# A chunked recurrence: the inverse from 32x32 blocks, heads in swapped halves, group norm on 128 partitions

## The chip, the cores and the metric

The kernel is one program on one core of a Trainium2 chip. The metric is the device time of one execution in microseconds (us); a run gives the median of its timed executions. All data are float32.

## The reference, cut to what matters

The program computes two transformer-like blocks for 256 tokens of width 1024. Only one layer of the first block is touched, a time mixing with 16 heads of 64 features. Per head it runs this recurrence over the tokens, then normalises each head's output, adds a bonus term and gates it:

```
state = state * w_t + (state @ -kk_t) (kk_t * a_t)' + v_t k_t'
y_t   = state @ r_t
yn    = (y - mean) * rsqrt(var + LNX_EPS) * lnx_w + lnx_b      (mean, var over each head's 64 features)
out   = ((yn + (sum(r * k * r_k)) * v) * g) @ w_o
```

## The kernel before

`rwkv()` works on four chunks of 64 tokens (`NCH`, `CHUNK`). 16 heads are held as 8 pairs m, with g = 0, 1 for the head of a pair, which takes partitions 0 to 63 or 64 to 127 (`half(g)`). Two blocks of code follow each other. The first (up to L1393) makes the operands: `ARs` (per pair and chunk a window w = 0 with the decayed -kk and w = 1 with r), `BKs` (w = 0 with kk*a, w = 1 with k), the values in `UV[64:128]`, `bonus`. The second (L1396 to L1715) is the recurrence, with an instruction list written out by hand for each engine; semaphores (`wait`) tie them together.

In the second block TensorE (PE) does for chunk c:

- `products` (L1455): all inner products of the chunk for each head, a 128x128 block (L1463), which VectorE (DVE) masks into `G` (L1647), and one more 64x64 product (L1469), masked into `NT[0]` (L1650). With N the strictly triangular 64x64 part of it, (I - N) has to be inverted.
- `power(c, j, q)` (L1473): the inverse as a product of (I + N^(2^j)). For j = 0 to 4 the powers N and their transposes are squared, 64x64 (L1485), and copied back by ScalarE (ACT, L1587); for j = 1 to 5 the running product X is multiplied by them (L1493) and DVE adds (L1662). q is one of two groups of four pairs, so that one group's copies run beside the other group's matmuls. The last X is `XF`.
- `values` (L1498): G's lower half times the values, 64 rows by 128 columns (L1502).
- in the body of chunk c: transposes of BK (L1524), the state's part of the right side (L1532), `products(c + 1)`, then u = XF times R (L1542), which ACT copies (L1603), y (L1550), which ACT copies to `Y` (L1610), and the new state (L1554), which DVE adds and decays (L1683, L1684).
- `z_turn` (L1506): the normalised outputs of the chunk before, turned back to features; DVE gates them (L1666).

The powers of chunk c + 1 are written in between, so PE has work while ACT and DVE handle chunk c. The group norm of chunk c (L1687 to L1714) is on DVE, interleaved with the `add_x` of chunk c + 1, on 64 partitions with 1024 elements each, since all tokens' outputs lie on partitions 64 to 127; ACT does the squares (L1616) and the root (L1621). ACT also copies the transposed N (`begin_at`, L1579).

A float32 matmul of the code leaves two MATMUL records in the trace and a transpose one: 16 matmuls of a `power` are x32.

Of the kernel before, what the change touches and what calls it, by code (L numbers as in the profile page):

```python
# [88 lines left out]
def build_program(nc, d, out):  # L89
    with ExitStack() as ctx:  # L90
# [16 lines left out]
        bonus = sb("bonus", [P, NCH, HEADS])  # L107
# [1046 lines left out]
        def rwkv():  # L1154
# [31 lines left out]

            def by_chunk(x):
                return x.rearrange("p m (c s) -> p m c s", c=NCH)
# [4 lines left out]
            with new_block() as block:  # L1193
# [8 lines left out]
                def _(dve):  # L1202
# [39 lines left out]
                    for f in range(2):  # L1242
                        dve.tensor_tensor(ARs[f][:, :, :, 1, :], two_chunks(rx, f), two_chunks(scratch, f), ALU.mult)
# [11 lines left out]
                    for f in range(2):  # L1255
                        dve.scalar_tensor_tensor(ARs[f][:, :, :, 0, :], two_chunks(kk, f), -1.0, two_chunks(sgm, f), ALU.mult, ALU.mult).then_inc(exp_used.up(), 1)
                    dve.wait_ge(exp_used.sem, exp_used.at(2))
                    dve.tensor_tensor(BKs[:, :, :, 0, :], by_chunk(ax), by_chunk(kk), ALU.mult)
                    dve.wait_ge(bonus_mm.sem, bonus_mm.at(1))
                    dve.tensor_copy(bonus[64:128].rearrange("p c a -> p (c a)"), bank(4)[64:128, 0:NCH * HEADS])  # L1260

                @block.tensor
                def _(pe):
# [68 lines left out]
                    for c in range(NCH):  # L1332
                        for m in range(KD):
                            last = pe.matmul(bank(4)[64:128, c * HEADS + 2 * m:c * HEADS + 2 * m + 2], xT[:, m, c * CHUNK:(c + 1) * CHUNK], pair, start=True, stop=True)
# [5 lines left out]
                def _(act):  # L1340
# [23 lines left out]
                    def copy_values(u):  # L1364
                        for t in range(T):
                            src = product(V_OUT + 2 * u + t)
                            for half in range(2):
                                o = UV[64:128, 2 * t + half, :, 4 * u:4 * u + 4, :].rearrange("p g m v -> p m g v")
                                ins = act.copy(o, src[64 * half:64 * half + 64, :].rearrange("p (m g v) -> p m g v", m=4, g=2))
# [21 lines left out]
                    act.wait_ge(exp_used.sem, exp_used.at(2))  # L1391
                    act.copy(BKs[:, :, :, 1, :], by_chunk(kx))
# [8 lines left out]
            NT = [blk(5)[:, i * 1024:(i + 1) * 1024].rearrange("p (m w s) -> p m w s", m=KD, w=2) for i in range(2)]  # L1401
            X = [spare[:, i * 512:i * 512 + 512].rearrange("p (m s) -> p m s", m=KD) for i in range(2)]
            R = spare[:, 1024:1536].rearrange("p (m v) -> p m v", m=KD)
            XF = spare[:, 1536:2048].rearrange("p (m s) -> p m s", m=KD)
            Y = blk(2)[64:128, 1024:2048]
            Z = blk(8)[64:128, 0:1024]
            W1 = blk(8)[64:128, 1024:2048]
            ST = mask.rearrange("p t s -> p (t s)").rearrange("p (m v) -> p m v", m=KD)
            POWERS = 5
# [9 lines left out]
            def half(g):  # L1419
# [1203 lines left out]
```

## Time and profile before

| | |
|---|---|
| median of 3 runs | 1875.41 us (1873.86 to 1875.72) |
| the profiled execution | 1868.42 us, its span 1866.8 us |
| PE, DVE, ACT busy | 1741.7, 957.2, 718.0 us |
| first block of `rwkv()` ends, recurrence begins | 477.25 us |
| recurrence ends, the next projection begins | 614.44 us |

The page gives the busy time of each engine; the timeline lists instructions in order of time, equal ones merged; the table of stretches gives busy times and the clock that TensorE was granted (1.00 is 2.4 GHz, 0.50 is 1.2 GHz). A matmul's record lasts about 0.22 us of which most overlaps with its neighbours, so the pace of a run of them is read from (merged time - one record) / (records - 1).

### The profile page before, as it was taken

The numbers are of one execution on the slowest core, as the hardware profiler recorded it, in microseconds if no ns is written. First come the engines' busy times: TensorE is split into PE (matmuls) and PEld (weight loads), VectorE is DVE, ScalarE is ACT, GpSimd is POOL, SyncE is SP. The second block draws the span as 40 slices with busy tenths as digits, with TensorE's granted clock in tenths as the row PEclk, the third lists the DMA queues.
The fourth block names the chain that finished last, engine by engine and source line by source line (L and its number), as shares of the span: only waits on it lengthen the run. The fifth ranks groups of instructions, "written<-read, shape, count | busy, mean of one in ns | idle before, by whom it ended". The sixth has DMA issues, their size and how long they took to land. (4 is left out here: it accounts for less than half of the span.)

```text
span 1866.8 us, 30841 instructions
## 1 busy us (share of the span) xinstructions
PE 1741.7 (93%) x12958; PEld 1372.5 (74%) x12958; DVE 957.2 (51%) x1947; ACT 718.0 (38%) x1322; POOL 0.2 (0%) x4
## 2 busy tenths in 40 slices
PE   8999999999997889999998999999978899999995
PEld 6778999786797789998787877555544688855553
DVE  6566556734376755567556755222223665713213
ACT  4465445323343444445546543111122454411111
POOL 0000000000000000000000000000000000000000
PEclk9999999999998899999999999999988999999998
DMA  7512454334000534543450435999962134499995
GB/s 309 226 62 98 180 203 158 110 136 158 25 3 2 214 125 178 203 146 125 163 198 20 161 147 195 423 425 426 423 292 90 46 113 158 156 418 425 424 426 229
DMA packets 34286, 374.34 MB, mean 201 GB/s; under 512 B 4944, under 2 KB 6096, under 8 KB 9568
## 3 DMA queue, kind: packets, MB, share of 16 engines
q1 hardware_dynamic: 30096, 362.51, 48.6%
q10 hardware_dynamic: 4048, 9.80, 1.6%
q8 instruction: 106, 1.74, 0.4%
q14 instruction: 36, 0.29, 0.0%
HBM read 371.25 MB, written 1.05 MB: 199 GB/s over the span
## 5 line engine op out<-in xcount | busy, mean ns | idle before, releaser
L1993 PE MATMUL ps<-ring,expert_inputs 128*64 128x256 f32 x2048 | 235.1, 382 | 7.7 <-DMA ring<-in_w_moe 7.7
L519 ACT CAST w_h<-ring 128x512 fp32r<-128x512 f32 x256 | 157.1, 622 | 140.0 <-PE ps L527 126.8
L522 DVE TENSOR_TENSOR w_l<-ring,w_h 128x512 fp32r<-128x512 f32 x256 | 172.4, 690 | 74.8 <-ACT w_h L519 72.3
L527 PE MATMUL ps<-ffn_x_h,ffn_w_h 128*128 128x256 f32 x704 | 201.3, 286 | 10.1 <-DVE ffn_w_l L522 9.9
L527 PE MATMUL ps<-ffn_x_l,ffn_w_h 128*128 128x256 f32 x704 | 200.5, 285 | 0.0
L527 PE MATMUL ps<-ffn_x_h,ffn_w_l 128*128 128x256 f32 x704 | 200.5, 285 | 0.0
L1993 PEld LDWEIGHTS ps<-ring,expert_inputs 128*64 128x64 f32 x2048 | 141.4, 137 | 77.4 <-DMA ring<-in_w_moe 8.8
L527 PE MATMUL ps<-w_h,x_h 128*128 128x512 f32 x416 | 163.6, 393 | 5.5 <-DVE w_l L522 5.5
L522 DVE TENSOR_TENSOR ffn_w_l<-ring,ffn_w_h 128x1024 fp32r<-128x1024 f32 x132 | 155.5, 1221 | 22.3 <-ACT ffn_w_h L519 22.3
L527 PE MATMUL ps<-w_h,x_l 128*128 128x512 f32 x416 | 162.0, 389 | 0.0
L527 PE MATMUL ps<-w_l,x_h 128*128 128x512 f32 x416 | 162.0, 389 | 0.0
L148 PE MATMUL ps<-ident 128*128 128x256 f32 x470 | 122.3, 409 | 33.4 <-PEq L2451 5.6
L519 ACT CAST ffn_w_h<-ring 128x1024 fp32r<-128x1024 f32 x132 | 131.2, 1045 | 37.7 <-PE ps L527 23.0
L527 PEld LDWEIGHTS ps<-ffn_x_h,ffn_w_h 128*128 128x128 f32 x704 | 136.5, 194 | 11.7 <-DVE ffn_w_l L522 10.9
L527 PEld LDWEIGHTS ps<-ffn_x_l,ffn_w_h 128*128 128x128 f32 x704 | 136.4, 194 | 0.8
L527 PEld LDWEIGHTS ps<-ffn_x_h,ffn_w_l 128*128 128x128 f32 x704 | 136.4, 194 | 0.0
L148 PEld LDWEIGHTS ps<-ident 128*128 128x128 f32 x470 | 92.3, 204 | 54.3 <-issue 41.7
L2121 ACT ACTIVATE routing<-ps 64x256 f32<-64x256 f32 x64 | 24.1, 376 | 279.3 <-PE ps L1993 279.3
L2245 DVE TENSOR_TENSOR routing<-routing,ps 64x256 f32<-64x256 f32 x64 | 27.2, 424 | 193.5 <-ACT routing L2121 193.3
L2016 PE MATMUL ps<-ring,routing 128*64 128x512 f32 x512 | 122.3, 598 | 0.8 <-DVE routing L2253 0.8
L527 PEld LDWEIGHTS ps<-w_h,x_h 128*128 128x128 f32 x416 | 78.1, 188 | 24.7 <-DVE w_l L522 5.1
L527 PEld LDWEIGHTS ps<-w_h,x_l 128*128 128x128 f32 x416 | 78.1, 188 | 16.3
(348 smaller groups left out, 2864.9 us busy)
## 6 DMA issues: line engine op xcount, KB each, us to landing
ring<-in_w_moe SPq DMA_DIRECT2D x64, 2048.0 KB, 14.4
ring<-in_w_proj SPq DMA_DIRECT2D x37, 2048.0 KB, 8.0
ring<-in_w_ffn SPq DMA_DIRECT2D x22, 3072.0 KB, 10.1
ring<-in_w_moe SPq DMA_DIRECT2D x64, 1024.0 KB, 16.0
rows<-in_ln_g ACTq DMA_DIRECT2D x6, 512.0 KB, 3.6
rows<-in_ln_b ACTq DMA_DIRECT2D x6, 512.0 KB, 5.3
ring<-in_w_b_in SPq DMA_DIRECT2D x1, 2496.0 KB, 19.2
ring<-in_w_lora SPq DMA_DIRECT2D x1, 2048.0 KB, 7.9
```

Of the source, the lines that this page charges most:

```text
L148: pe.matmul(bank(b)[:, 0:2 * P].rearrange("p (o f) -> p o f", o=2), ident[:], wide, start=True, stop=True, skip_group_check=True)
L519: act.copy(high, x).then_inc(ready.up(), 1)
L522: return dve.tensor_tensor(low, x, high.bitcast(F32), ALU.subtract)
L527: last = pe.matmul(out, a[x], b[y], start=start and n == 0, stop=stop and n == 2, skip_group_check=True)
L1993: last = pe.matmul(bank(0)[g * SLOTS_E:(g + 1) * SLOTS_E, 0:2 * P], x[:, k, e * SLOTS_E:(e + 1) * SLOTS_E], wg[:, g, k, :], start=(k == 0) ...
L2016: last = pe.matmul(bank(2)[c * SLOTS_E:(c + 1) * SLOTS_E, :], hids[:, f, :], wd[:, f, c * 512:(c + 1) * 512], start=(n % 2 == 0 and f == 0 ...
L2121: act.activation(sg[SLOTS_E:2 * SLOTS_E, :], bank(0)[0:SLOTS_E, 0:2 * P], ACT.Silu).then_inc(silu_done.up(), 1)
L2245: dve.tensor_tensor(hid_tok[up, :], sg[up, :], bank(0)[up, 0:2 * P], ALU.mult).then_inc(hid_made.up(), 1)
```

## The change

- In the first block `BKs`, `ARs` and the values are written so that for g = 1 the two windows and the two halves are swapped: the recurrence then has head g's N on partitions `half(g)` for both heads, and the values on `half(1 - g)`. An instruction that wrote all partitions becomes two that write 64.
- N is split in two 32x32 diagonal blocks (b = 0, 1) and one block below. `power` squares only the diagonal blocks, for j = 0 to 3 (`POWERS` = 4), as 32x32 matmuls, four for each pair (`sub(g, b)`); X is 32x32 too. `low` makes one product of the block below with the upper inverse and copies of it (L1543, L1544), ACT copies it (`copy_low`), `inverse` multiplies by the lower inverse (L1551), and ACT and DVE copy the results into `XF`. `products(c + 1)` and u now wait for these copies.
- `begin_at` goes: j = 0 reads `G` and `N0` in place. Two masks are made by six small ACT copies at the start.
- `values`, y and `z_turn` alternate between the halves; `values` comes after the last power. `z_turn` becomes 16 matmuls of 64x64 in place of 8 transposes.
- Y, W1 and Z have 128 partitions with 512 elements; the small rows of the group norm follow, and lnx_w and lnx_b come by four DMAs.
- The last chunk leaves out its transposes and its new state.

The diff, cut to its core:
```diff
-                                ins = act.copy(o, src[64 * half:64 * half + 64, :].rearrange("p (m g v) -> p m g v", m=4, g=2))
+                            for part in range(2):
+                                x = src[half(part), :].rearrange("p (m g v) -> p m g v", m=4, g=2)
+                                for g in range(2):
+                                    ins = act.copy(UV[half(1 - g), 2 * t + part, g, 4 * u:4 * u + 4, :], x[:, :, g, :])
                             ins.then_inc(evac.up(), 1)
...
-            POWERS = 5
+            gms = [gm, rows[:, 0, 512:640]]
+            eye = sin0.rearrange("p t f -> p (t f)")[:, CHUNK:CHUNK + SUB]
+            lnx = [rows[:, i, 0:512] for i in range(2)]
+            POWERS = 4
...
-                        for q in range(2):
-                            if c:
-                                pe.wait_ge(x_added[q].sem, x_added[q].at(POWERS * c))
+                        if c:
+                            for copied, count in inverse_copied(c - 1):
+                                pe.wait_ge(copied.sem, count)
...
+                        tiles = [(m, m % GROUP, g, b) for m in range(GROUP * q, GROUP * (q + 1)) for g in range(2) for b in range(2)]
                         if j < POWERS:
-                            for m in range(GROUP * q, GROUP * (q + 1)):
-                                i = m % GROUP
-                                for w in range(2 if j < POWERS - 1 else 1):
-                                    for g in range(2):
-                                        last = pe.matmul(nt_out(q)[half(g), i, w, :], nt[half(g), m, 1 - w, :], nt[half(g), m, w, :], start=True, stop=True)
+                            for w in range(2 if j < POWERS - 1 else 1):
+                                for m, i, g, b in tiles:
+                                    x = operands(c, j, m, g, b)
+                                    last = pe.matmul(nt_out(q)[sub(g, b), i, w, :], x[1 - w], x[w], start=True, stop=True)
                             last.then_inc(powers_ready[q].up(), 1)
...
+                            for m, i, g, b in tiles:
+                                last = pe.matmul(x_out(q)[sub(g, b), i, :], NT[j % 2][sub(g, b), m, 0, :], X[j % 2][sub(g, b), m, :], start=True, stop=True)
...
+                    def low(c, q):
+
+                        pe.wait_ge(x_added[q].sem, x_added[q].at(POWERS * (c + 1)))
+                        if c == 0:
+                            wait(pe, "masks_made", 2)
+                        for m, i, g in heads_of(q):
+                            pe.matmul(inv_out(q)[sub(g, 0), i, half_cols(0)], XF[sub(g, 0), m, half_cols(1)], eye[sub(g, 0), :], start=True, stop=True)
+                            last = pe.matmul(low_out(q)[sub(g, 1), i, :], before(c, g)[sub(g, 0), m, half_cols(1)], XF[sub(g, 0), m, half_cols(1)], start=True, stop=True)
+                        last.then_inc(low_ready.up(), 1)
+
+                    def inverse(c, q):
+
+                        pe.wait_ge(act_out.sem, low_copied(c, q))
+                        for m, i, g in heads_of(q):
+                            last = pe.matmul(inv_out(q)[sub(g, 0), i, half_cols(1)], LOW[sub(g, 1), m, :], XF[sub(g, 1), m, half_cols(1)], start=True, stop=True)
+                        last.then_inc(inv_made.up(), 1)
...
-                        for g in range(2):
-                            for m in range(KD):
-                                last = pe.matmul(bank(VY + g)[:, m * 64:(m + 1) * 64], G[c % 2][64:128, g, m, :], UV[64:128, c, g, m, :],
+                        for m in range(KD):
+                            for g in range(2):
+                                last = pe.matmul(bank(VY + g)[:, m * 64:(m + 1) * 64], G[c % 2][half(1 - g), g, m, :], UV[half(1 - g), c, g, m, :],
...
-                        for m in range(KD):
-                            last = pe.transpose(bank(M_BANK)[:, m * CHUNK:(m + 1) * CHUNK], Z[:, m * P:(m + 1) * P], ident[64:128, 64:128])
+                        for m, i, g in ALL:
+                            last = pe.matmul(bank(M_BANK)[half(g), m * CHUNK:(m + 1) * CHUNK], Z[half(1 - g), m * HD:(m + 1) * HD], ident[half(1 - g), half(1 - g)], start=True, stop=True)
...
+                    def last_power(c):
+                        for q in range(2):
+                            power(c, POWERS, q)
+                        values(c)
+                        for q in range(2):
+                            low(c, q)
...
-                        for m in range(KD):
+                        for m in range(KD if ahead else 0):
...
+                        for q in range(2):
+                            inverse(c, q)
                         if ahead:
+                            wait(pe, "bk_copied", 2 * c + 2)
                             products(c + 1)
...
+                        for m, i, g in ALL:
+                            last = pe.matmul(bank(VY + g)[half(1 - g), m * 64:(m + 1) * 64], G[c % 2][half(g), g, m, half(1 - g)], UV[half(g), c, g, m, :],
...
+                            act.wait_ge(low_ready.sem, low_ready.at(2 * c + q + 1))
+                            for g in range(2):
+                                ins = act.copy(LOW[sub(g, 1), pairs(q), :], low_out(q)[sub(g, 1)])
+                            ins.then_inc(act_out.up(), 1)
...
-                        begin_at(c + 1, 0)
+                        for q in range(2):
+                            act.wait_ge(inv_made.sem, inv_made.at(2 * c + q + 1))
+                            act.copy(XF[sub(0, 0), pairs(q), :], inv_out(q)[sub(0, 0)]).then_inc(act_out.up(), 1)
...
+                            dve.tensor_tensor(N0[:, pairs(q), :], by_pair(bank(M_BANK))[:, pairs(q), :], wide_l, ALU.mult).then_inc(n["an_begun"].up(), 1)
+                        wait(dve, "g_masked", 4 * c + 4)
+                        wait(dve, "an_begun", 2 * c + 2)
+                        for g in range(2):
+                            for b in range(2):
+                                x = before(c, g) if b else N0
+                                ins = dve.tensor_tensor(X[1][sub(g, b)], x[sub(g, b), :, half_cols(b)], wide_i[sub(g, b)], ALU.add)
+                        ins.then_inc(n["x_begun"].up(), 1)
...
-                        o = (XF if j == POWERS else X[(j + 1) % 2])[:, pairs(q), :]
+                        o = XF[:, pairs(q), half_cols(1)] if j == POWERS else X[(j + 1) % 2][:, pairs(q), :]
                         dve.tensor_tensor(o, X[j % 2][:, pairs(q), :], x_out(q), ALU.add).then_inc(x_added[q].up(), 1)
...
+                        for q in range(2):
+                            dve.wait_ge(inv_made.sem, inv_made.at(2 * c + q + 1))
+                            dve.tensor_copy(XF[sub(1, 0), pairs(q), :], inv_out(q)[sub(1, 0)]).then_inc(dve_out.up(), 1)
...
                         add_x(c + 1, 2, 0)
+                        add_x(c + 1, 2, 1)
                         dve.wait_ge(sig("squares_ready").sem, sig("squares_ready").at(c + 1))
-                        step(dve.tensor_reduce(sm, rows3(W1), AX, ALU.add))
-                        add_x(c + 1, 2, 1)
-                        dve.tensor_scalar(stat[64:128, 16:32], sm, 1.0 / HD, LNX_EPS, ALU.mult, ALU.add).then_inc(sig("mean_square").up(), 1)
+                        step(dve.tensor_reduce(sm, by_pair(W1), AX, ALU.add))
                         add_x(c + 1, 3, 0)
+                        dve.tensor_scalar(stat[:, 16:24], sm, 1.0 / HD, LNX_EPS, ALU.mult, ALU.add).then_inc(sig("mean_square").up(), 1)
+                        add_x(c + 1, 3, 1)
...
-                        step(dve.tensor_tensor(W1, W1, rows[64:128, 1, :], ALU.add))
                         add_x(c + 1, 4, 0)
+                        add_x(c + 1, 4, 1)
+                        step(dve.tensor_tensor(W1, W1, lnx[1], ALU.add))
                         dve.wait_ge(sig("row_root").sem, sig("row_root").at(c + 1))
```

PE, the powers of chunk 1 (before) and of chunk 0 (now): L1485 and L1526 square, L1493 and L1534 multiply X.

```order
L1485 MATMUL ps<-arena_7 64x64 x16
L1493 MATMUL ps<-ring,arena_7 64x64 x8
L1485 MATMUL ps<-arena_7 64x64 x16
L1493 MATMUL ps<-ring,arena_7 64x64 x8
L1485 MATMUL ps<-arena_7 64x64 x8
```

```order
L1526 MATMUL ps<-arena_7 32x32 x32
L1534 MATMUL ps<-ring,arena_7 32x32 x16
L1526 MATMUL ps<-arena_7 32x32 x32
L1534 MATMUL ps<-ring,arena_7 32x32 x16
L1526 MATMUL ps<-arena_7 32x32 x16
```

Each step has twice as many matmuls, of a quarter of the size, and there is one step fewer.

PE, from the end of chunk 1's powers to u of chunk 1: the first piece is before (L1502 is `values`, L1524 the transposes, L1532 the state's part, L1463 and L1469 `products`, L1542 u), the second is now (L1543 and L1544 `low`, L1551 `inverse`).

```order
L1502 MATMUL ps<-arena_8,arena_0 128x64 x16
L1493 MATMUL ps<-ring,arena_7 64x64 x16
L1524 MATMUL ps<-ident,arena_7 128x128 x8
L1532 MATMUL ps<-mask,ring 128x64 x16
L1463 MATMUL ps<-ring,arena_7 128x128 x8
L1469 MATMUL ps<-arena_7,ring 64x64 x16
L1463 MATMUL ps<-ring,arena_7 128x128 x8
L1542 MATMUL ps<-ring 64x64 x16
```

```order
L1543 MATMUL ps<-sin,ring 32x32
L1544 MATMUL ps<-ring,arena_0 32x32
L1586 MATMUL ps<-ident,arena_7 128x128 x8
L1594 MATMUL ps<-mask,ring 128x64 x16
L1551 MATMUL ps<-ring,arena_7 32x32 x16
L1497 MATMUL ps<-ring,arena_7 128x128 x8
L1503 MATMUL ps<-arena_7,ring 64x64 x16
L1497 MATMUL ps<-ring,arena_7 128x128 x8
L1607 MATMUL ps<-ring 64x64 x16
```

`inverse` stands between the state's part and the products, which wait for the copies of what it made; the pair L1543, L1544 comes 16 times.

ACT in the same place and on to Y: before (L1597 copies the transposes, L1599 R, L1579 `begin_at`, L1603 u, L1587 the powers, L1610 Y), and now (L1649 `copy_low`, L1672 the new copies into `XF`).

```order
L1597 COPY arena_0<-ps 128x512 x2
L1599 COPY ring<-ps 64x512
L1579 COPY arena_7<-arena_0 64x4x64 x2
L1603 COPY arena_8<-ps 64x512 x2
L1579 COPY arena_7<-arena_0 64x4x64 x2
L1587 COPY arena_7<-ps 128x512
L1610 COPY arena_0<-ps 64x8x64 x2
```

```order
L1649 COPY arena_7<-ps 32x128 x4
L1667 COPY arena_0<-ps 128x512 x2
L1669 COPY ring<-ps 64x512
L1672 COPY ring<-ps 32x256 x2
L1675 COPY arena_8<-ps 64x512 x2
L1641 COPY arena_7<-ps 128x256
L1681 COPY arena_0<-ps 64x512 x2
```

Two short copies of `XF` stand behind R's; the copies of the powers have half the elements.

## Rows read from the trace of the kernel before

**Rows 1.** Page, section 1: busy us (share of the span) x instructions.

```profile
PE 1741.7 (93%) x12958; PEld 1372.5 (74%) x12958; DVE 957.2 (51%) x1947; ACT 718.0 (38%) x1322; POOL 0.2 (0%) x4
```

**Rows 2.** Busy time, granted clock, DMA by stretch: prologue, three chunks, last chunk.

```profile
477.25:499.00 21.75, 20.62 (x545) 19.93 (x545) 8.54 (x19) 7.05 (x14) 0.00 (x0) 1.00 0.14 51
499.00:527.55 28.55, 26.71 (x651) 25.36 (x649) 18.47 (x33) 13.07 (x24) 0.00 (x0) 0.98 0.01 3
527.55:557.33 29.78, 29.43 (x690) 28.03 (x689) 22.12 (x36) 12.10 (x23) 0.00 (x0) 0.96 0.01 3
557.33:587.36 30.03, 29.68 (x690) 28.33 (x688) 21.98 (x36) 12.10 (x23) 0.00 (x0) 0.95 0.02 4
587.36:614.44 27.08, 11.41 (x156) 10.42 (x152) 16.77 (x21) 5.14 (x9) 0.00 (x0) 0.63 0.00 1
```

**Rows 3.** Groups of instructions by line, 475 to 615 us: busy, mean ns | idle before.

```profile
L1485 PE MATMUL ps<-arena 64*64 64x64 f32 x1152 | 40.1, 219 | 1.9 <-ACT arena L1579 1.0 <-ACT arena L1587 0.7
L1493 PE MATMUL ps<-ring,arena 64*64 64x64 f32 x640 | 25.7, 223 | 0.0
L1587 ACT COPY arena<-ps 128x256 f32<-128x256 f32 x8 | 3.0, 373 | 3.2 <-PE ps L1485 3.2
```

**Rows 4.** Timeline of the first two bodies: start us, us, engine, line, operation.

```profile
506.51 2.07 PE L1550 MATMUL ps<-arena,arena 64*64 64x64 f32 x32 [0.35 <-ACT arena L1603]
...
508.51 1.15 PE L1554 MATMUL ps<-arena,arena 128*64 128x64 f32 x32
...
509.60 2.08 PE L1485 MATMUL ps<-arena 64*64 64x64 f32 x64
...
522.13 3.78 PE L1502 MATMUL ps<-arena,arena 64*128 64x64 f32 x32
...
527.55 1.97 PE L1524 MATMUL ps<-ident,arena 128*128 128x128 f32 x8
...
529.45 2.03 PE L1532 MATMUL ps<-mask,ring 64*128 64x64 f32 x32
...
531.52 0.58 ACT L1599 COPY ring<-ps 64x512 f32<-64x512 f32 x1 [1.39 <-PE ps L1532]
```

**Rows 5.** PE in windows of 10 ns: matmuls then in flight (x).

```profile
482.84:482.85 0.01, 0.00 (x0) 1.00 0.00 0
482.86:482.87 0.01, 0.01 (x2) 1.00 0.00 0
...
483.03:483.04 0.01, 0.01 (x6) 1.00 0.00 0
...
483.09:483.10 0.01, 0.01 (x8) 1.00 0.00 0
```

**Rows 6.** Stretches at half clock (same columns as rows 2).

```profile
526.10:529.50 3.40, 3.40 (x42) 2.95 (x36) 2.19 (x4) 0.59 (x1) 0.00 (x0) 0.50 0.00 0
...
594.40:614.40 20.00, 6.64 (x74) 6.05 (x71) 13.10 (x16) 2.33 (x4) 0.00 (x0) 0.50 0.00 1
```

**Rows 7.** Timeline of the last chunk.

```profile
587.37 1.09 PE L1524 MATMUL ps<-ident,arena 128*128 128x128 f32 x8
...
593.80 3.21 PE L1550 MATMUL ps<-arena,arena 64*64 64x64 f32 x32 [1.27 <-ACT arena L1603]
...
597.04 1.06 ACT L1610 COPY arena<-ps 64x512 f32<-64x512 f32 x2 [3.30 <-PE ps L1550]
...
600.40 1.22 DVE L1687 TENSOR_REDUCE stat<-arena 64x16 f32<-64x1024 f32 x1
...
612.28 1.08 PE L1509 MATMUL ps<-ident,arena 64*128 64x64 f32 x8 [12.32 <-DVE arena L1714]
```

**Rows 8.** Timeline around the seam of the two blocks of `rwkv()`.

```profile
475.75 1.17 ACT L1369 COPY arena<-ps 64x512 f32<-64x512 f32 x2 [5.70 <-PE ps L1296]
...
477.28 1.16 PE L1463 MATMUL ps<-ring,arena 64*128 64x128 f32 x16 [1.57 <-PEq L1193]
...
478.56 1.29 DVE L1647 TENSOR_TENSOR arena<-ps,cos 128x512 f32<-128x512 f32 x2 [18.20 <-PE ps L1463]
```

More of the change, by code:

```diff
@@ L1390, in _ @@
                     copy_values(0)
-                    act.wait_ge(exp_used.sem, exp_used.at(2))
-                    act.copy(BKs[:, :, :, 1, :], by_chunk(kx))
+                    act.wait_ge(exp_used.sem, exp_used.at(4))
+                    for g in range(2):
+                        act.copy(BKs[half(g), :, :, 1 - g, :], by_chunk(kx)[half(g)])
                     copy_values(1)
@@ L1450, in _ @@
                 def _(sp):
-                    sp.dma_start(rows[:, 0, :], d["lnx_w"].rearrange("(o f) -> o f", o=1).broadcast_to([P, D])).then_inc(c_in.up(16), 16)
-                    sp.dma_start(rows[:, 1, :], d["lnx_b"].rearrange("(o f) -> o f", o=1).broadcast_to([P, D])).then_inc(c_in.up(16), 16)
+                    for i, x in enumerate((d["lnx_w"], d["lnx_b"])):
+                        by_half = x.rearrange("(o m g v) -> o g m v", o=1, m=KD, g=2)
+                        for g in range(2):
+                            sp.dma_start(by_pair(lnx[i])[half(1 - g)], by_half[:, g].broadcast_to([64, KD, HD])).then_inc(c_in.up(16), 16)
                 @block.tensor
@@ L1515, in _ @@
                             power(0, j, q)
[L1516 to L1519 removed]
+                    last_power(0)
                     for c in range(NCH):
                         ahead = c + 1 < NCH
[L1523 removed]
+                        for m in range(KD if ahead else 0):
                             last = pe.transpose(bank(NT_BANK + m // 4)[:, (m % 4) * P:(m % 4 + 1) * P], BK(m, c), ident[:])
@@ L1565, in _ @@
                                     power(c + 1, j, q)
-                            values(c + 1)
-                            for q in range(2):
-                                power(c + 1, POWERS, q)
+                            last_power(c + 1)
                     wait(pe, "z_gated", NCH - 1)
@@ L1573, in _ @@
                 def _(act):
-                    def begin_at(c, q):
-                        if c == NCH:
-                            return
-                        wait(act, "g_masked", 4 * c + 2 * q + 2)
-                        for g in range(2):
-                            ins = act.copy(NT[0][half(g), pairs(q), 1, :], G[c % 2][0:64, g, pairs(q), 0:64])
-                        ins.then_inc(n["at_begun"].up(), 1)
                     def copy_powers(c, j, q):
@@ L1593, in _ @@
                             copy_powers(0, j, q)
+                    copy_low(0)
                     for c in range(NCH):
-                        for f in range(2):
+                        for f in range(2 if c + 1 < NCH else 0):
                             wait(act, "bk_turned", 2 * c + f + 1)
@@ L1666, in gate @@
                         dve.tensor_tensor(xT[:, :, c * CHUNK:(c + 1) * CHUNK], by_pair(bank(M_BANK)), gT[:, :, c * CHUNK:(c + 1) * CHUNK], ALU.mult).then_inc(n["z_gated"].up(), 1)
+                    for g in range(2):
+                        ins = dve.memset(XF[sub(g, 1), :, half_cols(0)], 0.0)
+                    step(ins)
                     dve.wait_ge(masks_in.sem, masks_in.count)
+                    wait(dve, "masks_made", 2)
                     begin(0)
```

173 lines of the change are left out of this document (92 added, 81 removed).

## The prediction

> **What bounds the kernel now.** I read the page first: TensorE (PE) is busy 93% of the span, DVE 51%, ACT 38% [rows 1]. Then the table of stretches, since the change lies in one stage of 137 us, 477.25 to 614.44. Its prologue takes 21.75 us and its three full chunks 28.55, 29.78 and 30.03 us, mean 29.45; in the full chunks PE is busy all but 0.4 us or so of each later stretch, and DMA moves next to nothing [rows 2]. The last 27 us are another case: PE is busy 11.4 of them and DVE 16.8. So the chunks are bound by how fast PE takes the small matmuls, and the last one by a chain through DVE. Before the stage ends nothing later can start, and the stages behind it keep their lengths: I take what the stage gains or loses as the kernel's.
>
> **Pace of the matmuls.** The trace has 1152 + 640 records of the powers [rows 3], 448 a chunk, 224 matmuls of the code. 64 records of alternating halves take 2.08 us: (2.08 - 0.22) / 63 = 29.5 ns a record, 59 ns a matmul. Where all matmuls use the same rows (y, L1550), (2.07 - 0.22) / 31 = 60 ns a record; so two halves of the array work side by side and each keeps 60 ns. With 128 columns of weights, one half alone takes (3.78 - 0.27) / 31 = 113 ns a record (`values`), alternating halves (2.03 - 0.27) / 31 = 57 [rows 4]. The narrow windows show that after a wait two matmuls are in flight within the same 20 ns, and from then on two more every 60 ns: 2, 6, 8 in flight [rows 5]. The start of a second half costs the first nothing.
>
> **The powers.** Now there are 2 x 176 = 352 matmuls of 32x32 a chunk, with `low` and `inverse` 400, at a price s that the trace doesn't show. From below: a 32x32 record should hold its part of the array for half of 60 ns, and with four parts side by side a matmul (two records) costs 2 x 30 / 4 = 15 ns. A middle price is 30 ns, if the second record of one matmul has to follow its first before the next part may start. From above 59 ns, since no two matmuls of the code follow each other faster anywhere in the stage. 13.2 us (224 x 59) become 6.0, 12.0 or 23.6 us. I take 20 ns, 8.0 us: nearer to the lower end because of rows 5, above it because `low` and `inverse` use two parts only. That is -5.2 us a chunk.
>
> **The rest of a full chunk.** (1) `values` goes from 3.78 to the 2.03 of L1532, -1.8; y from 2.07 to about 1.15 as L1554, -0.95 [rows 4]. (2) `z_turn`: 8 records of some 0.1 become 32 at 30 ns, +0.4. (3) After `values` the clock falls to 0.50 for 3.4 us [rows 6]; 8 transposes then take 1.97 us [rows 4] and not 1.09 [rows 7]. With both halves busy I expect this in fewer chunks, -1.0. (4) A new wait: `inverse` must be copied before `products(c + 1)`. ACT has R's copy (0.58, [rows 4]) ahead of two short copies, for which I take 0.3 each, below the 0.37 of 128x256 [rows 3]; PE meanwhile had only `inverse` itself, and its whole stream stands behind the wait. +1.1. `copy_low` is covered by the transposes and the state's part, 3 us; without that cover it would cost 0.9. (5) Changes of matmul shape: L1554 starts at 508.51 and at 30 ns a record would hand over at 509.47; L1485 starts at 509.60 [rows 4], 0.1 us later than in a run of equal shape. Some seven more such changes, +0.7. (6) Between u and y PE waits 0.35 us for ACT's copies although a `power` fills the gap [rows 4]; a shorter `power` leaves 0.3 more, and the chain of copies and DVE steps between powers may show another 0.3: +0.6. ACT's `begin_at` is gone and the copies of powers are 0.37 in place of 0.59; DVE loses half of eight norm steps; both engines have room (18 to 22 and 13 of 29 us busy, [rows 2]), so I cost that at nothing, covered by PE's matmuls; if PE fell under DVE's 18 us of work, DVE would be next. Sum: -5.2 - 1.8 - 0.95 + 0.4 - 1.0 + 1.1 + 0.7 + 0.6 = -6.15, a chunk of 23.3 us; three are -18.5.
>
> **The prologue.** -5.2 and -1.8 as above, -1.0 for `begin_at`, +0.5 for the chain, +0.3 for the six copies that make the masks (they lie beside `products(0)`): -7.2.
>
> **The last chunk.** No transposes, but the inverse's wait: -0.6. y at half clock takes 3.21 us on one half [rows 7]; alternating, half of it: -1.5. DVE's first norm step starts at 600.40, though the second copy of Y ends at 598.10, since the state's two steps stand before it: they go, -2.3. The norm has seven steps of 64x1024 at 1.22 us [rows 7]; 128x512 takes 0.65 (half of 1.29, [rows 8]); seven times 0.55 and 0.4 for the square: -4.2. `z_turn` at half clock: +0.7. Sum -7.9; PE waits 12.32 us for this chain [rows 7].
>
> **The first block.** Split writes double some DVE and ACT steps, and BKs' copy. DVE is idle for 18.20 us before its first step of the recurrence, so some 7 us more are hidden; ACT's last copies (two of 0.58 ending at 476.92, [rows 8]) become four shorter ones, +0.5 on the path. The four DMAs of lnx_w and lnx_b have short pieces but are wanted only 15 us after they are issued: nothing.
>
> **Sum.** -18.5 - 7.2 - 7.9 + 0.5 = -33.1 us against the profiled execution (1868.42 us, 1.6 around its span), which lies 7.0 below the median; the same difference from the median 1875.4 gives **1842 us**.
>
> **Other prices of s.** At 15 ns a full chunk is -7.5 and the prologue -8: 1837 us. At 30 ns -2.75 and -3.7: -8.3 - 3.7 - 7.4 = -19.4, 1856 us. The sum is zero near 43 ns.
>
> The windows show two parts starting together, and no more can be seen in this kernel. The Trainium skill (TensorE: Matmul & The Clock Gate, Part 3, The mechanism) says that small parts of the array run concurrently with starts some 4 ns apart; rows 5 agree for two parts. By it alone s would be the 15 ns above, and the time 1837 us.
>
> **Rivals.** (a) *PE takes no more than one matmul per 59 ns*, whatever its size: what limits it is taking instructions, not the array. For it: no closer pace in 1792 records, and 59 is also what two halves would give, so the trace can't tell. Against it: after a wait two matmuls start together. Powers, `low` and `inverse` then cost 23.6 us, +10.4; with (1), (2), (3), (4), (5) and 1.2 us of waits that vanish behind the longer stream, a chunk is +7.6, three +22.8; the prologue +7.9; the last chunk and the seam -7.4: +23.3, **1899 us**. It decides from 43 ns on. The Trainium skill (TensorEngine Tiling (Array Packing), Instruction Overhead) speaks for this side: each matmul has an overhead of about 60 cycles, and one should not take a tiling factor from a dimension that is already small. An estimate from that page is 25 ns a record at 2.4 GHz, and 50 ns a matmul if both records pay it, near 1885 us; no run here shows it for 32 columns. (b) *The clock stays at 0.50 in the chunks*, since short matmuls with waits between them keep PE less busy: the last chunk runs so [rows 6]. Work like the transposes then takes 1.8 times as long; some 17 us of a chunk are PE's, +14 each, which gives 1842 + 42 + 10 = 1894 us. (c) *The chain, not PE, bounds the new chunk*: each power needs PE, ACT's copy and back, and DVE's additions stand behind norm steps. It would hold a chunk at 26 to 27 us: 1853 us. (d) The change doing less than it says, such as half of the tiles side by side: s = 30, 1856 us.
>
> **How the numbers follow.** Forecast (s from 15 to 25 ns) 0.42, its own range 1832 to 1850; (c) or (d) 0.22; (a) with its milder form at 50 ns 0.29; (b) 0.05; the rest 0.02. The predicted time is the forecast's, 1842. The range must leave out no more than 2 in 10: from 1830 (15 ns and no half clock) to 1892, which takes in the milder part of (a). Within 0.2% (about what a measurement of this kernel can tell) is 1871.7 to 1879.2 us: 0.04. Faster 0.65, slower 0.31.
>
> **What would show it.** The 32x32 matmuls of L1526 closer than 15 ns a record; full chunks of 22 to 25 us; a wait of about 1 us before L1497 with ACT's L1672 as its end; `values` at 57 ns a record and no half clock behind it; the norm steps at 0.65 to 0.69 us; PE's wait before the last `z_turn` some 7 us shorter. I am wrong if L1526 keeps 29 ns a record, or if the chunks show half clock.

## The result: 23 us slower, and the profile after

The changed kernel takes 1897.59 us (median of 4, 1895.54 to 1901.58); the kernel before took 1874.63 us beside it. The ratio is 1.0127, 95% interval 1.0107 to 1.0147. The prediction of 1842 us, range 1830 to 1892, had the wrong sign and a range that doesn't hold the time. The profiled execution has a span of 1893.7 us. Page, section 1, answers to [rows 1]:

```profile
PE 1738.7 (92%) x14486; PEld 1366.7 (72%) x14486; DVE 943.2 (50%) x1952; ACT 708.9 (37%) x1335; POOL 0.2 (0%) x4
```

PE has 1528 records more and is busy 3 us less. The stage, cut at the same places as in [rows 2] (prologue, three full chunks, last chunk; the columns are the same, the clock is the number before the last two):

```profile
476.14:503.15 27.01, 19.09 (x865) 17.54 (x865) 8.55 (x21) 4.16 (x16) 0.00 (x0) 0.64 0.10 23
503.15:537.41 34.26, 25.41 (x1006) 23.36 (x1000) 15.04 (x33) 10.29 (x25) 0.00 (x0) 0.65 0.01 4
537.41:577.18 39.77, 30.44 (x1071) 28.09 (x1065) 16.91 (x36) 9.31 (x24) 0.00 (x0) 0.67 0.01 4
577.18:617.04 39.86, 31.16 (x1071) 28.65 (x1064) 16.99 (x36) 9.29 (x24) 0.00 (x0) 0.63 0.01 3
617.04:639.86 22.82, 12.31 (x200) 11.57 (x193) 9.52 (x17) 5.23 (x13) 0.00 (x0) 0.50 0.01 2
```

The stage takes 163.7 us in place of 137.2. Against [rows 2] the prologue is +5.3, the chunks are +5.7, +10.0 and +9.8, the last chunk is -4.3. Two columns tell how. PE, which was busy all but 0.4 us of a later chunk, now stands still for 9 us of it, and the granted clock is 0.63 to 0.67 where it was 0.95 to 0.98. The groups of PE in the stage, against [rows 3]:

```profile
L1526 PE MATMUL ps<-arena 32*32 32x32 f32 x1280 | 22.0, 217 | 16.3 <-issue 16.3
L1534 PE MATMUL ps<-ring,arena 32*32 32x32 f32 x1024 | 20.6, 228 | 12.0 <-issue 11.3 <-DVE ring L1723 0.5
L1560 PE MATMUL ps<-arena,arena 64*128 64x64 f32 x128 | 14.7, 421 | 0.0
L1497 PE MATMUL ps<-ring,arena 64*128 64x128 f32 x128 | 13.2, 365 | 3.9 <-PEq L1196 1.9 <-DVE ring L1752 1.2 <-ACT ring L1672 0.7
L1594 PE MATMUL ps<-mask,ring 64*128 64x64 f32 x96 | 11.0, 421 | 0.0
```

The idle time lies before the 32x32 matmuls of the powers, 27.6 us of it with "issue" as its end: PE waited for no engine, no semaphore and no data that the profile shows. Here is one such piece of the first full chunk in narrow stretches:

```profile
517.90:519.00 1.10, 1.06 (x120) 1.06 (x121) 0.00 (x0) 0.36 (x1) 0.00 (x0) 1.00 0.06 15
...
520.00:521.30 1.30, 0.00 (x0) 0.00 (x0) 0.00 (x0) 0.00 (x0) 0.00 (x0) 0.91 0.00 0
521.30:522.40 1.10, 1.00 (x76) 1.00 (x79) 0.00 (x0) 0.37 (x1) 0.00 (x0) 0.50 0.00 0
522.40:523.30 0.90, 0.90 (x71) 0.79 (x60) 0.83 (x2) 0.00 (x0) 0.00 (x0) 0.50 0.08 18
523.30:525.10 1.80, 0.02 (x3) 0.00 (x0) 0.07 (x1) 0.89 (x2) 0.00 (x0) 0.50 0.00 0
525.10:526.20 1.10, 1.08 (x81) 1.07 (x84) 0.29 (x1) 0.00 (x0) 0.00 (x0) 0.50 0.00 0
526.20:527.20 1.00, 0.85 (x64) 0.72 (x56) 0.22 (x2) 0.37 (x1) 0.00 (x0) 0.50 0.06 16
527.20:528.50 1.30, 0.00 (x0) 0.00 (x0) 0.67 (x2) 0.00 (x0) 0.00 (x0) 0.50 0.00 0
```

At clock 1.00, 120 records start in 1.10 us: 9 ns a record, 18 ns a matmul. So the array takes the new matmuls as cheaply as predicted. But after a burst comes a pause in which no engine's work is awaited, and with each burst one transfer (18 GB/s for 0.9 us, 16 KB). The queue that it belongs to, in the window 477 to 620 us, first of the kernel after, then of the kernel before:

```profile
q8 instruction: 32, 0.52, 1.4%
```

```profile
q8 instruction: 21, 0.34, 1.0%
```

Each packet is 0.52 MB / 32 = 16 KB of instructions. Cut at the ends of the stage itself, the queue has 33 packets after and 21 before. Bursts begin at 521.39, 525.12 and 528.58, one batch apart.

The other reading is of the wait before `products` and of the last chunk (timeline):

```profile
539.31 3.68 PE L1594 MATMUL ps<-mask,ring 64*128 64x64 f32 x32
...
543.60 0.79 ACT L1672 COPY ring<-ps 32x256 f32<-32x256 f32 x2
543.65 0.80 DVE L1752 COPY ring<-ps 32x256 f32<-32x256 f32 x2
...
544.60 2.08 PE L1497 MATMUL ps<-ring,arena 64*128 64x128 f32 x16 [0.61 <-DVE ring L1752]
...
636.77 1.98 PE L1567 MATMUL ps<-ident,arena 64*64 64x64 f32 x32 [7.46 <-DVE arena L1789]
```

The rhs matmuls of L1594, 2.03 us in [rows 4], take 3.68 at half clock. The wait for the inverse's copies is there. Here it ends with DVE's copy, at 544.45, just after ACT's at 544.39; of the three waits of the stage (0.6 to 0.7 us each) two end with DVE's copy and one with ACT's L1672. The wait before the last `z_turn` is 7.46 in place of 12.32 [rows 7].

### The profile page after: what moved, and what is told of

It reads as the page before. It is cut to its first block and busy times, and to the rows that moved or that the text cites. A ratio compares the mean times of both kernels' runs of the same rounds, so it can differ in the third digit from the quotient of the medians.

```text
span 1893.7 us, 33918 instructions
## 1 busy us (share of the span) xinstructions
PE 1738.7 (92%) x14486; PEld 1366.7 (72%) x14486; DVE 943.2 (50%) x1952; ACT 708.9 (37%) x1335; POOL 0.2 (0%) x4
## 5 line engine op out<-in xcount | busy, mean ns | idle before, releaser
L527 PE MATMUL ps<-ffn_x_h,ffn_w_h 128*128 128x256 f32 x704 | 201.4, 286 | 10.1 <-DVE ffn_w_l L522 9.8
L527 PE MATMUL ps<-w_h,x_h 128*128 128x512 f32 x416 | 163.7, 394 | 6.7 <-DVE w_l L522 6.7
L527 PEld LDWEIGHTS ps<-ffn_x_h,ffn_w_h 128*128 128x128 f32 x704 | 136.4, 194 | 11.6 <-DVE ffn_w_l L522 10.9
## 6 DMA issues: line engine op xcount, KB each, us to landing
ring<-in_w_moe SPq DMA_DIRECT2D x64, 2048.0 KB, 14.7
ring<-in_w_ffn SPq DMA_DIRECT2D x22, 3072.0 KB, 10.1
```

The source lines that it names most:

```text
L527: last = pe.matmul(out, a[x], b[y], start=start and n == 0, stop=stop and n == 2, skip_group_check=True)
```

## The experiments

Two theories: **supply** (PE gets its instructions in batches of 16 KB, one per 3.45 us or more, which 64 float32 matmuls use up) and **clock** (half clock makes the wide matmuls of a chunk slower, and is a loss of its own). The rival of the first is a fixed price for each matmul.

### The price of the small matmuls by itself

```diff
+for k in range(384):                        # before products(0)
+    r = slice(32 * (k % 4), 32 * (k % 4) + 32)
+    pe.matmul(spare_bank[r, 0:32], ident[r, 0:32], ident[r, 0:32], ...)
+# the same with 64 columns; then 64x64 on two halves, 64 columns
```

> The kernel before, with three runs of matmuls put ahead of the recurrence's first product, 384 each, none waiting for anything: 32x32 on four parts with 32 columns (L1515), the same with 64 columns (L1518), and 64x64 on two halves with 64 columns (L1521). Supply theory (instructions reach PE in batches of 16 KB, 64 float32 matmuls, one each 3.45 us at best): the first two take the same, 384 x 54 ns = 20.7 us, in bursts at 15 and 30 ns a matmul with pauses between them, and a 16 KB fetch ahead of each burst; the third takes 384 x 59 = 22.7 us without pauses. Per-matmul theory (each matmul costs a fixed 54 to 59 ns): the same totals, but evenly spaced, no pauses. Array theory: 5.8, 11.5 and 22.7 us.

Measured: 1937.26 us (one execution). The three runs as stretches, and part of the first in the timeline:

```profile
477.70:498.90 21.20, 10.08 (x769) 9.44 (x773) 0.00 (x0) 0.00 (x0) 0.00 (x0) 0.61 0.17 53
498.90:520.82 21.92, 13.65 (x775) 12.55 (x775) 0.00 (x0) 0.00 (x0) 0.00 (x0) 0.91 0.02 4
520.86:543.73 22.87, 22.87 (x776) 22.67 (x770) 0.00 (x0) 0.00 (x0) 0.00 (x0) 1.00 0.02 4
```

```profile
477.70 2.28 PE L1515 MATMUL ps<-ident 32*32 32x32 f32 x249 [1.57 <-PEq L1193]
484.43 1.93 PE L1515 MATMUL ps<-ident 32*32 32x32 f32 x128 [4.46 <-issue]
488.16 1.93 PE L1515 MATMUL ps<-ident 32*32 32x32 f32 x128 [1.80 <-issue]
491.62 1.93 PE L1515 MATMUL ps<-ident 32*32 32x32 f32 x128 [1.53 <-issue]
495.07 1.93 PE L1515 MATMUL ps<-ident 32*32 32x32 f32 x128 [1.53 <-issue]
```

384 matmuls take 21 to 23 us whatever their size, but in two ways. The 64x64 ones follow each other at 59.6 ns without a pause. The 32x32 ones start with 249 records in one piece, 2.28 us: after the wait about two batches of instructions lay ready, and for these the price is that of the array. Then they come in bursts of exactly 128 records, that is 64 matmuls with their weight loads, 256 instructions, and a batch starts every 3.45 or 3.73 us: 54 to 58 ns a matmul. With the 16 KB of a packet an instruction has 64 bytes. The time lies in the pauses (10.1 us busy of 21.2), and doubling the columns only fills part of them. So the array is not the limit.

Nor does the pace of the batches follow the clock: it is the same in the first run, whose later bursts ran at half clock, and in the second, where it was 1.00 from its second burst on. The packets can be counted too: over the whole kernel the instruction queue has 106 before and 124 here, and the 18 more are the 1152 matmuls at 4 instructions each, 256 to a packet. Whether it is bytes of instructions or a count of matmuls this run can't tell.

### Half the instructions for each matmul

```diff
+half_price = ident[:].bitcast(mybir.dt.bfloat16)
+for k in range(768):                        # before products(0)
+    pe.matmul(spare_bank[r, 0:32], half_price[r, 0:32], half_price[r, 0:32], ...)
+for k in range(384):
+    pe.matmul(spare_bank[r, 0:128], ident[r, 0:32], ident[r, 0:128], ...)
```

> Kernel before, with two runs of matmuls put ahead of its first products that nothing reads: 768 of 32x32 with 32 columns in bf16 (one weight load and one matmul instruction each), then 384 of 32x32 with 128 columns in float32 (two of each). Theory (PE is supplied one batch of 16 KB, 256 instructions, in no less than 3.45 us): the bf16 run is 6 batches, 20.7 us, 27 ns a matmul, with pauses between bursts; the second is also 6 batches, 20.7 us at least, but the array needs 4 x 128 columns x 2 passes on four parts, 57 to 60 ns a matmul at clock 1.00: 22 to 23 us without pauses once the clock is up. The total is 1873.6 + 44 = 1917. Rival (a fixed price of 54 ns or so for each matmul whatever its instructions): the bf16 run takes 41 us, the total 1937.

Measured: 1918.61 us (one execution), within 2 us of the sum by supply.

```profile
481.07:502.85 21.78, 7.13 (x767) 6.60 (x771) 0.00 (x0) 0.00 (x0) 0.00 (x0) 0.57 0.16 52
502.85:526.20 23.35, 23.35 (x771) 23.00 (x775) 0.00 (x0) 0.00 (x0) 0.00 (x0) 0.89 0.02 4
```

```profile
492.16 1.22 PE L1516 MATMUL ps<-ident 32*32 32x32 bf16 x128 [2.50 <-issue]
495.62 1.22 PE L1516 MATMUL ps<-ident 32*32 32x32 bf16 x128 [2.23 <-issue]
```

A bf16 matmul is one weight load and one matmul instruction, so a batch holds 128 of them, and 768 take the time that 384 in float32 took: 28 ns each. The same batch, the same 3.46 to 3.73 us, half the price a matmul: what is limited is instructions, 256 per batch, and not matmuls. The queue has 118 packets, 12 more than before, as 768 x 2 + 384 x 4 instructions fill. The packet counts fit one size for all of them, so their number and their bytes can't be told apart. The second run streams 128 columns, needs 61 ns a matmul from the array, and has no pause. Within a burst a bf16 matmul follows the last after (1.22 - 0.185) / 127 = 8 ns at half clock. The Trainium skill (TensorEngine Tiling (Array Packing), Instruction Overhead) gives about 60 cycles for each matmul, which was the milder form of rival (a); these bursts don't show it.

### The 32x32 blocks taken out again

The change without its smaller blocks: `POWERS` is 5 again, the powers are of 64x64, `low` and `inverse` are gone. Swapped halves, alternating `values` and y, the norm on 128 partitions and the shortened last chunk stay. With one more power, the places of DVE's and ACT's steps for the last powers among the norm steps differ a little too.

```diff
-            POWERS = 4
+            POWERS = 5
-last = pe.matmul(nt_out(q)[sub(g, b), i, w, :], x[1 - w], x[w], ...)
+last = pe.matmul(nt_out(q)[half(g), i, w, :], x[1 - w], x[w], ...)
```

> The changed kernel with the inverse taken back to whole 64x64 blocks (POWERS = 5, no low, no inverse, j = 0 still reads G in place); swapped halves, alternating values and y, group norm on 128 partitions and the shorter last chunk stay. Supply theory: a chunk needs 224 matmuls at 59 ns in place of 400 at 54, PE never pauses and the clock stays up; full chunks of 25 to 27 us, 1848 to 1858 us in all, 20 or more below before. If what made the change slow lay in the swapped halves or the new order of values, this kernel would stay near 1890.

Measured: 1859.6 us, ratio to before 0.9925 (0.9896 to 0.9954). It is faster than both, and 38.0 us faster than after: that is the price of the blocks with all that hangs on them (pauses, clock, the inverse's wait), where the prediction had -20.8 for the powers (four times -5.2) and +3.3 for three waits. Its chunks take 25.6, 28.3 and 31.0 us. One thing in them can be mended; the timeline of the third:

```profile
581.54 1.25 PE L1522 MATMUL ps<-ring,arena 64*64 64x64 f32 x32 [1.35 <-DVE ring L1683]
```

### Wide matmuls as filler

In the kernel after, a 128x128 matmul of 192 columns that nothing reads ahead of each 8 small ones from the third power on, 24 a chunk, to see the chunks with a busy array. PE also waits once a chunk for the state's update, whose bank the fillers write.

```diff
+if j > 1 and (g, b) == (0, 0) and i % 2 == 0:
+    pe.matmul(bank(STEP_BANK)[:, 0:192]..., ident[:], wide_96_twice, ...)
```

> The changed kernel with a wide matmul (128x128 weights, 192 columns, result thrown away) after every 8 small ones from j = 2 on, 24 a chunk. They need 12% more instructions but put 0.32 us of array work each where PE paused. Clock theory (the loss is half clock, not supply): the clock stays at 1.00 there, values and the state's part go from 3.7 to 2.0 us, total down by 8 to 12 us against the changed kernel. Supply theory: the powers get longer by the 12%, some 2 us a chunk; with the clock back the sum is between -6 and +2 us against the changed kernel, and it stays slower than before.

Measured: 1982.73 us, ratio 1.0583 (1.0553 to 1.0613). This missed what both theories expected.

```profile
489.60:534.00 44.40, 43.67 (x658) 30.62 (x646) 5.16 (x13) 4.85 (x14) 0.00 (x0) 0.50 0.01 2
```

```profile
506.61 0.44 PE L1534 MATMUL ps<-arena 32*32 32x32 f32 x16
506.98 1.01 PE L1507 MATMUL ps<-ident 128*128 128x192 f32 x2
507.92 0.44 PE L1534 MATMUL ps<-arena 32*32 32x32 f32 x16
```

PE is now busy 43.67 of 44.40 us, and the clock is 0.50 all through. A group of 8 small matmuls and its filler takes 1.31 us, 0.94 of it for the filler and the change of shape to and from it; 96 fillers are 90 us, about the 85 lost. So the fillers are paid about in full, though the pauses before the small matmuls shrink from 27.6 to 9.1 us, and the total speaks for neither theory. And a PE that the profile shows as busy doesn't have the full clock for that. Why the clock stayed down here isn't settled; the next run fills the array in another way.

### The same instructions with twice the columns

```diff
-last = pe.matmul(nt_out(q)[sub(g, b), i, w, :], x[1 - w], x[w], ...)
+last = pe.matmul(nt_two(q)[sub(g, b), :, i, w, :], x[1 - w], twice(x[w]), ...)
```

and the same for X: the second 32 columns are a copy in free columns of the bank.

> Kernel after, with one change: the 32x32 matmuls of the powers (L1526 and L1534) stream 64 columns in place of 32, the wanted 32 and a copy of them into free columns of the same bank. Instructions, waits and copies stay the same in number and order; only the columns that the array has to stream are doubled. In the run of the three kinds of tiles the second kind (32x32, 64 columns) took 21.9 us for 384 matmuls where the first took 21.2, and the clock, 0.50 up to 502.7, was 1.00 from there on. Theory (instruction supply sets the pace of the small matmuls, and the half clock is a loss of its own, that comes from an array that is idle for most of the time): the pauses are shorter by what the matmuls take longer, the batches keep their 3.45 us, the clock is at 1.00 in most of the chunks, and the wide work between (values 3.68 -> 2.03, products, rhs, u, y, state, transposes, some 8 us of a chunk that lies wholly at half clock) is faster: 10 to 25 us less than 1897.6, about 1880; full chunks of 30 to 34 us in place of 34.3 to 39.8. Rival 1 (supply alone; the wide work is hidden behind the fetches, so the clock costs nothing): within 4 us of 1897.6 although the clock is up. Rival 2 (the array sets the pace, 30 ns a matmul in place of 15): 5 to 6 us more a chunk, 1915 or more.

Measured: 1886.48 us, ratio 1.0069 (1.0045 to 1.0093), 11.1 us less than after. The full chunks, and three groups of PE:

```profile
505.20:537.45 32.25, 23.41 (x1009) 21.43 (x1000) 14.86 (x33) 10.25 (x26) 0.00 (x0) 0.95 0.02 4
537.45:574.19 36.74, 30.06 (x1071) 27.32 (x1065) 15.73 (x35) 9.18 (x23) 0.00 (x0) 0.86 0.02 4
574.19:610.35 36.16, 27.37 (x1072) 24.99 (x1064) 17.62 (x38) 9.15 (x25) 0.00 (x0) 0.94 0.02 4
```

```profile
L1535 PE MATMUL ps<-arena 32*32 32x64 f32 x1280 | 25.1, 215 | 14.3 <-issue 14.3
L1543 PE MATMUL ps<-ring,arena 32*32 32x64 f32 x1024 | 21.7, 215 | 11.1 <-issue 11.0
...
L1569 PE MATMUL ps<-arena,arena 64*128 64x64 f32 x128 | 9.3, 296 | 0.1
```

Twice the columns in the powers' matmuls make the kernel faster. The pauses are nearly the same (25.3 us in place of 27.6), but the clock is 0.86 to 0.95. The gain is in the wide work: `values` (L1560, now L1569) 14.7 to 9.3 us, and with L1594, L1497 and L1503 some 9.7 us, about the stage's 9.5. So half clock is a loss of its own, 11 us or somewhat more (the chunks are still at 0.86 to 0.95, and the last one at 0.57), and most of the rest is not the clock.

### Fewer instructions for the same powers

X stands beside the transposed power, and one matmul of 64 columns makes both where they share their weights: 336 small matmuls a chunk in place of 400.

```diff
+if merged:   # j in (1, 2)
+    pe.matmul(nt_out(q)[sub(g, b), i, 1:3, :], NT[j % 2][sub(g, b), m, 0, :],
+              NT[j % 2][sub(g, b), m, 1:3, :], ...)
```

> The changed kernel with X stored beside the transposed powers, so that for j = 1 and 2 one matmul of 64 columns does what two of 32 did: 288 + 48 matmuls a chunk in place of 352 + 48, the same work for the array; DVE's addition waits for ACT's copy (same PSUM bank). Supply theory: 64 x 54 ns = 3.5 us less a chunk, 14 us less in all against the changed kernel (10 to 15 if the longer chain shows). Array or clock theory: no gain, rather 1 to 4 us more.

Measured: 1881.99 us, ratio 1.0046 (1.0029 to 1.0063), 15.6 us less than after. By supply alone 64 matmuls in four inverses are 4 batches, 14 us, and the instruction queue does have 114 packets in place of 118. The chunks are 30.7, 34.5 and 35.8 us at clocks of 0.70 to 0.74, so a little of the gain can be the clock.

### Both together

```diff
 # the merged version, and where a power or X is not merged:
+pe.matmul(nt_out(q)[sub(g, b), i, w:w + 2, :], x[1 - w], twice(x[w]), ...)
+pe.matmul(x_two(q)[sub(g, b), :, i, :], ..., twice(X[j % 2][sub(g, b), m, :]), ...)
```

> Kernel after with both edits: X beside the transposed powers where they share weights, 336 small matmuls a chunk in place of 400 (alone: 15.6 us less than after), and 64 columns streamed in place of 32 by the other matmuls of the powers (alone: 11.1 us less). If instruction supply and the half clock are the two causes of after's loss and they add up, the sum is 1897.6 - 26.7 = 1870.9, and since the merging alone had already raised the clock a little (0.952 to 0.956), somewhat less is left: 1868 to 1877, clock 0.97 or more, pauses of PE fewer than in after but still there (336 + 152 matmuls a chunk by 54 ns is 26 us). Rival 1 (the pauses and the clock are one and the same loss, so the second edit adds nothing): 1879 to 1884. Rival 2 (without pauses 32x32 tiles win after all): below 1853.1, the best version with whole blocks.

Measured: 1871.25 us, ratio 0.9982 (0.9966 to 0.9997); expected from the sum were 1870.9. The two losses add up. In the stage:

```profile
503.38:531.12 27.74, 21.47 (x881) 19.53 (x873) 14.86 (x33) 10.38 (x26) 0.00 (x0) 0.95 0.02 4
531.12:565.18 34.06, 28.37 (x942) 25.93 (x937) 16.27 (x36) 9.18 (x23) 0.00 (x0) 0.84 0.02 4
565.18:596.66 31.48, 26.52 (x945) 24.31 (x937) 16.13 (x36) 9.03 (x24) 0.00 (x0) 0.89 0.01 4
```

Of the 38.0 us that the blocks cost, 26.3 are undone. The last 11.7 stay. This version still has 336 small matmuls a chunk where whole blocks have 224, and PE stands still for 5 to 6 us a chunk; no run takes these 11.7 apart.

### The best version

Whole blocks, with DVE's additions of the fourth X ahead of norm steps that don't need them.

```diff
 ins = dve.tensor_tensor(by_pair(W1)[r], UV[r, c, g, :, :], w, ALU.mult)
+if g == 0:
+    add_x(c + 1, 4, 0)
 step(ins)
+add_x(c + 1, 4, 1)
 step(dve.tensor_tensor(W1, W1, lnx[1], ALU.add))
-add_x(c + 1, 4, 0)
```

> The version with whole 64x64 blocks (1859.6), with DVE's additions of the fourth X put ahead of the norm steps that it doesn't need: the first behind one of the two bonus products, the second ahead of the addition of lnx_b. In that version's trace PE waits 1.36 us, 521.05 to 522.51, in each of three chunks for the first of them, which is ready at 520.23 and stands behind DVE's steps up to 521.90. Theory: the wait goes down to the 0.3 us or so by which the second addition is late, -1.1 us a chunk, 1856 to 1857. Rival (the wait only moves, to values or to the last X behind the later norm steps, or to the last z_turn): 1859 to 1860.

Measured: 1853.14 us, ratio 0.9893 (0.9875 to 0.9911), 3 us better than expected.

```profile
479.93:499.56 19.63, 18.84 (x545) 18.15 (x545) 8.82 (x18) 6.17 (x14) 0.00 (x0) 1.00 0.13 30
499.56:524.14 24.58, 23.14 (x650) 22.06 (x648) 15.18 (x31) 11.09 (x20) 0.00 (x0) 1.00 0.01 3
524.14:550.31 26.17, 25.45 (x715) 24.44 (x713) 17.44 (x35) 10.12 (x19) 0.00 (x0) 1.00 0.02 4
550.31:576.70 26.39, 25.51 (x714) 24.47 (x713) 17.66 (x35) 10.13 (x19) 0.00 (x0) 1.00 0.02 4
576.70:596.19 19.49, 8.59 (x161) 8.08 (x161) 9.52 (x17) 3.77 (x8) 0.00 (x0) 0.71 0.00 1
```

The wait of 1.35 us went down to 0.4, as expected. What came beside it is the clock: the third chunk, 0.87 in the version before this one, is at 1.00, and takes 4.6 us less. That the shorter wait is what kept the clock up was not tried.

### All versions side by side

| version | small matmuls a chunk | full chunks, us | clock in them | stage, us | kernel, us |
|---|---|---|---|---|---|
| before | 224 | 28.6, 29.8, 30.0 | 0.98, 0.96, 0.95 | 137.2 | 1874.6 |
| after | 400 | 34.3, 39.8, 39.9 | 0.65, 0.67, 0.63 | 163.7 | 1897.6 |
| after, twice the columns | 400 | 32.3, 36.7, 36.2 | 0.95, 0.86, 0.94 | 154.2 | 1886.5 |
| after, X merged | 336 | 30.7, 34.5, 35.8 | 0.72, 0.70, 0.74 | 147.7 | 1882.0 |
| after, both | 336 | 27.7, 34.1, 31.5 | 0.95, 0.84, 0.89 | 136.4 | 1871.3 |
| after, with fillers | 400 | 54.4, 61.0, 61.9 | 0.59, 0.58, 0.58 | 247.6 | 1982.7 |
| after with whole blocks | 224 | 25.6, 28.3, 31.0 | 1.00, 0.96, 0.87 | 124.6 | 1859.6 |
| the same, additions earlier | 224 | 24.6, 26.2, 26.4 | 1.00, 1.00, 1.00 | 116.3 | 1853.1 |

The kernel before took 1873.4 to 1873.7 us beside the versions of the lower rows.

## Why the prediction was wrong, step by step

**The price s: the step that failed.** I took 20 ns for a 32x32 matmul, from two matmuls that start together in [rows 5], with 59 ns as the upper bound. The price of the array is right: 18 ns in a burst at full clock. But PE gets 64 float32 matmuls per 3.45 to 3.73 us, 54 to 58 ns each, and 176 matmuls more a chunk have no room in that. The error was to take the narrow windows as evidence about a long run. They show two records starting after a wait, when instructions lie ready (about 125 matmuls' worth in the 32x32 run), and say nothing on how fast these come. The trace of before had a hint: 21 packets of 16 KB in the stage, and in the runs of powers one every 3.9 to 4.6 us, while 64 matmuls at 59 ns take 3.8 us. Its powers ran 2 to 9% above a floor that no row of it names, so it never showed as idle time. The prediction's own sum has its zero at 43 ns; at 54 it says slower. (Its figures for 15 and 30 ns don't quite follow from its terms, which give 1834 and 1858 in place of 1837 and 1856; nothing hangs on that.)

**A count that would have told it.** A full chunk has 400 small matmuls and, by the code, 136 others, 8 of them transposes with half the instructions: 2128 instructions, 8.3 batches, 28.7 us at 3.45 us a batch and 29.9 at 3.6, which is nearer to the mean of the long runs, against the 29.45 of before. So even with an array that costs nothing and the full clock the chunks had at best 0.8 us each to gain. (The expectation of the run with both edits counted 152 others; 136 is right, and its floor is 25.2 us at 3.45.) With twice the columns, at a clock of 0.86 to 0.95, a chunk came to 32 to 37 us: what of the wide work lies ahead of a batch and what beside it I can't separate.

**Rival (a)** said 1899 us with 59 ns a matmul, and 1897.59 was measured. It named taking instructions as the limit, and that is right in kind. Its form is wrong, since matmuls do follow closer than 59 ns, in bursts, and part of its agreement is luck: it had the prologue at +7.9 (measured +5.3) and the last chunk and seam at -7.4 (-4.3 for the chunk), with 22.8 for three chunks (25.5), of which the clock made a good part. Its 0.29 was too low for a row that couldn't tell 59 ns of array from 59 ns of supply; the rows for s were silent on supply.

**Step (3) and rival (b): the clock.** I expected less half clock, -1.0 a chunk, and gave lasting half clock 0.05. It came, together with the pauses and not by itself: 0.63 to 0.67 in the chunks, and 11 us of the loss, not the 52 of rival (b). (b) let 14 us a chunk grow by it; that much of that work was waiting for instructions anyway would explain it, but was not tested. Why the clock fell is only known in part: with the same pauses and twice the columns it came back, and with PE filled by wide matmuls it did not.

**Steps (1) and (2).** `values` alternating takes 2.00 us in the best version, as forecast from L1532, and y 1.15 with whole blocks, as forecast from L1554; in the kernel after, 3.68 for `values` at half clock hid that.

**Steps (4) to (6).** The new wait has its place as predicted. Its end is ACT's L1672 in one chunk and DVE's L1752 in two; the prediction had looked only at ACT, but DVE has the same two copies behind its own copy of R. It is 0.6 to 0.7 us a chunk in the kernel after, where `inverse` itself takes 1.06 us at half clock beside the copies, and 1.0 in the mean of the run with both edits; the copies take 0.36 to 0.42 where I had 0.3. So 1.1 was about right. (5) and (6) can't be told apart in chunks that stand still for other reasons. (6) had its counterpart with whole blocks: the chain of X stood behind norm steps for 1.35 us.

**Rivals (c) and (d)** decided nothing: DVE is busy 15 to 17 us of a longer chunk, and all tiles did go side by side.

**The other parts held.** Without the blocks the prediction's terms for the prologue are -2.0 (-1.8 - 1.0 + 0.5 + 0.3); the best version has -2.1. A chunk without powers and inverse, and without (5) and (6), had -3.35 (-1.8 - 0.95 + 0.4 - 1.0); it has -3.7 in the mean. The last chunk had -7.9; it has -7.6, with the wait before the last `z_turn` at 7.7 in place of 12.32 [rows 7] and norm steps at 0.69. In the kernel after the last chunk gains only 4.3: of the 3.3 us in between, 2.5 are its rhs matmuls (3.68 for 2.0) and u (1.97 for 1.15) at half clock, the rest lies beside the inverse and its copies. The +0.5 of the first block can't be read: the stage begins between 476.1 and 481.3 us in these kernels, by what lies ahead of it.

## What to carry to other kernels

Count instructions before you cut a matmul into smaller ones: here PE was given 16 KB, 64 float32 matmuls or 128 bf16 ones with their weight loads, per 3.45 to 3.73 us, and a long run of matmuls that would come closer than 54 to 58 ns (28 in bf16) is bound by that, however little the array does. Only the first two batches after a wait are there at once. Look for idle time that ends with "issue", for bursts of equal length, and at the packets of the instruction queue; in the runs here a matmul that does more columns for the same instruction was free up to that floor, and merging two was a gain. And when one part of a change loses, look at the others by themselves: here they were worth 14 us, and 20 with DVE's additions moved.

## What the runs showed of the hardware that I had not expected

- The pauses form a loop. In the 32x32 run a burst of 128 records starts every 3.45 or 3.73 us; there and in the kernel after (bursts at 521.39, 525.12 and 528.58) a transfer of 16 KB begins about 1.1 us after a burst's start, takes 0.9 to 1.2 us, and the next burst starts 1.2 to 1.6 us after it has landed. Why nothing of this overlaps is open.
- A long run starts with some 249 records in one piece, in float32 and in bf16 alike, about two batches, before the first pause (4.46 and 5.18 us).
- The stalls are invisible to the busy share: the page has PE busy 92% after and 93% before.
- A PE busy for 43.67 of 44.40 us ran at a granted clock of 0.50 all through, with 32x32 tiles and 128x128 tiles in turn.
- Doubling the streamed columns of 2816 of the stage's records, with every instruction, wait and copy kept, made the kernel 11 us faster.
